# Mixing stage: the scores of a later item between the transposes and the products with the values

## What is computed

```python
s_c = jnp.einsum('bqgrd,bcgd->bqgrc', qg, k_cmp) * scale          # compressed blocks
p_c = masked_softmax(s_c, ...); o_c = einsum(p_c, v_cmp)
_, idx = lax.top_k(score, topk)                                    # 8 blocks of 64 keys per query
p_s = masked_softmax(s_s, (kpos <= qpos)...);  o_s = einsum(p_s, values of those blocks)
p_w = masked_softmax(s_w, wmask);              o_w = einsum(p_w, values of the window of 256)
o = g[..., 0:1] * o_c + g[..., 1:2] * o_s + g[..., 2:3] * o_w
```

## Time and profile before

| | us |
|---|---|
| median of 3 runs | 4092.09 |
| lowest and highest | 4089.07, 4095.11 |
| the profiled execution | 4092.92 |
| its span | 4091.1 |
| TensorE busy in it | 3914.1 (96%) |
| VectorE, GpSimd, ScalarE busy | 2043.8, 1694.0, 1114.4 |

### The profile page before, as it was taken

One profiled execution on the slowest core, in us unless ns is written; L12 is line 12 of the kernel. 1 busy time (PEld: TensorE's weight loads), 2 busy tenths in 40 slices (PEclk: granted clock), 3 DMA queues, 4 the chain that ended last, 5 costly groups with the idle time before them and its releaser, 6 DMA issues. The chain is left out here.

```text
span 4091.1 us, 89056 instructions
## 1 busy us (share of the span) xinstructions
PE 3914.1 (96%) x36904; PEld 3583.7 (88%) x36904; DVE 2043.8 (50%) x4689; ACT 1114.4 (27%) x2470; POOL 1694.0 (41%) x2284
## 2 busy tenths in 40 slices
PE   8998999989999999999999989999899999999997
PEld 8987888876689999999899878888666999999997
DVE  6587544447545424415456864444575454144253
ACT  3153233337731000000212532323477211000001
POOL 5533221126764434434355321221367644344442
PEclk9998999989999999999999999999899999999998
DMA  3254432220032131131323443332200311311312
GB/s 131 87 166 164 115 84 66 84 97 4 16 100 79 46 112 66 42 135 39 111 93 102 149 166 100 82 85 68 95 7 13 123 63 45 135 42 59 118 42 93
DMA packets 201957, 350.13 MB, mean 86 GB/s; under 512 B 72930, under 2 KB 135650, under 8 KB 200674
## 3 DMA queue, kind: packets, MB, share of 16 engines
q1 hardware_dynamic: 201554, 344.44, 26.6%
HBM read 253.18 MB, written 95.90 MB: 85 GB/s over the span
## 5 line engine op out<-in xcount | busy, mean ns | idle before, releaser
L2628 POOL CAST wr_hi<-wr_raw 128x256 fp32r<-128x256 f32 x584 | 263.7, 452 | 906.0 <-PE ps L2663 900.6
L2630 POOL TENSOR_TENSOR wr_lo<-wr_raw,wr_hi 128x256 fp32r<-128x256 f32 x584 | 548.1, 938 | 46.7
L2663 PE MATMUL ps<-xh,wr_hi 128*128 128x384 f32 x2064 | 453.5, 328 | 0.0
L2663 PE MATMUL ps<-xh,wr_lo 128*128 128x384 f32 x2064 | 453.2, 327 | 0.0
L2663 PE MATMUL ps<-xl,wr_hi 128*128 128x384 f32 x2064 | 452.9, 327 | 0.0
L1382 POOL TENSOR_TENSOR rc_CT<-rc_AT,rc_masks 128x256 f32<-128x256 f32 x192 | 138.7, 742 | 602.2 <-DVE rc_AT L1417 451.6
L2663 PEld LDWEIGHTS ps<-xh,wr_hi 128*128 128x128 f32 x2064 | 349.1, 188 | 0.3
L2663 PEld LDWEIGHTS ps<-xl,wr_hi 128*128 128x128 f32 x2064 | 349.0, 188 | 0.0
L2663 PEld LDWEIGHTS ps<-xh,wr_lo 128*128 128x128 f32 x2064 | 348.6, 188 | 0.0
L2716 ACT ACTIVATE de_c<-de_c 128x1088 f32<-128x1088 f32 (+1 forms) x44 | 49.1, 1116 | 1098.2 <-DVE de_c L2812 1098.2
L2663 PE MATMUL ps<-de_mixh,wr_hi 128*128 128x384 f32 (+3 forms) x1440 | 321.6, 331 | 7.9 <-DVE de_mixl L2751 7.9
(11 more groups left out here) (460 smaller groups left out, 8034.3 us busy)
## 6 DMA issues: line engine op xcount, KB each, us to landing
sa_kvp<-in_cache SPq DMA_DIRECT2D x128, 256.0 KB
scr_xres<-de_x SPq DMA_DIRECT2D x56, 544.0 KB, 2.7
de_x<-scr_xres SPq DMA_DIRECT2D x56, 544.0 KB, 3.7
wr_raw<-in_w_gate SPq DMA_DIRECT2D x42, 512.0 KB, 3.5
wr_raw<-in_w_up SPq DMA_DIRECT2D x42, 512.0 KB, 3.5
rc_arbk<-scr_arbk SPq DMA_DIRECT2D x32, 512.0 KB, 4.8
wr_raw<-in_w_down SPq DMA_DIRECT2D x32, 512.0 KB, 3.6
pr_raw<-in_w_rw SPq DMA_DIRECT2D x28, 512.0 KB, 4.2
```

The costliest lines, as they stand in the source:

```text
L2628: pool.tensor_copy(hi[:, k, :], raw[:, k, :]).then_inc(w_hi, 1)
L2630: pool.tensor_tensor(lo[:, k, :], raw[:, k, :], f32(hi[:, k, :]), ALU.subtract).then_inc(w_ready, 1)
L2663: m = pe.matmul(ps[:, (bank + b) * BANK:(bank + b) * BANK + cols], w[rows, k, :], x[rows, k, o:o + cols], start=(k == 0 and i == 0), stop= ...
```

## The change

The one edit is in TensorE's loop. `scores(i + LAG)` stood behind `values(i - 1)` and stands ahead of it:

```diff
@@ -2136,10 +2136,10 @@
             for i in range(-LAG, NI + 2):
                 if 0 <= i < NI:
                     transposes(i)
+                if i + LAG < NI:
+                    scores(i + LAG)
                 if 0 <= i - 1 < NI:
                     values(i - 1)
-                if i + LAG < NI:
-                    scores(i + LAG)
                 yield
```

## The result

| | kernel before | changed kernel |
|---|---|---|
| median of the runs, us | 4093.61 (10 runs, 4086.54 to 4098.73) | 4103.68 (10 runs, 4099.30 to 4106.57) |
| ratio of the times | | 1.0023, 95% interval 1.0013 to 1.0032 |
| profiled execution: span, us | 4091.1 | 4104.8 |

The changed kernel is slower by 0.23%, 10.1 us by the medians and 5.3 to 13.1 by the interval. I measure it from the first score group behind the gap at its start to the end of the last product with the values. Behind that score group every step depends on the one before it, and the moment at which the clock first rose, a little ahead of that score group and not the same in each execution, is left out.

What follows compares the result with a forecast made beforehand. The prediction took the mixing stage to be bound by TensorE's own work. Its terms, 6.5 + 1.9 + 3.4 - 4.0 = +7.8 us on 4092.09, gave 4099.9 us, with a range of 4091 to 4108 for 8 in 10.

Steps and rivals of the forecast that it cites:

- Term A: Diagonal steps: array switches from causal product to values and values to transposes cost 0.13 in 25 steps, +6.5 us both layers.
- The zero price of the new switches: All steps: the new neighbours transposes to scores and scores to values cost nothing in sum over the old ones.
- Rival 4: All steps: the new switches are dear, 0.06 each over 150 steps, 4109 us; plain step above 2.46; chance 0.18.
- the ceiling of 0.17: Stage start: transposes ahead of scores last 0.97, 0.17 over the plain 0.80, an upper bound for that switch.
- Term B: Stage start: first values leave the shadow of a mask wait, next scores are 0.95 late, +1.9 us both layers.
- Term C: Stage start: behind a gap of 3.1 us TensorE's clock falls to half for 3.4 us, +3.4 us both layers.
- Term D: Mixing stage: transposes' waits for GpSimd and L2128's wait for ScalarE shorten, 2.0 per layer, -4.0 us both layers.
- The 7.0 stay: Mixing stage: scores' waits for VectorE's masks, 7.0 us per layer, stay apart from the first of them.
- (1): Stage start: the clock doesn't fall, or falls in one layer only, 4096.5 to 4098 us; chance 0.20.
- (2): Mixing stage: nothing moves, switches are covered by remaining waits and the start is made good, 4092 to 4094 us; chance 0.13.
- (3): Mixing stage: faster, since earlier scores feed VectorE early and mask waits go as well, about 4081 us; chance 0.09.

Runs made afterwards that it cites:

- first step in the old order: Changed kernel, but in the first step that has values they stand ahead of the scores as before: 4095.00 us against 4092.72 of the kernel before, ratio 1.0007.
- two products: Changed kernel with two added products, whose result nobody reads, in the gap ahead of the first moved scores of each layer: 4098.41 us, one execution.
- two kernels without C: Causal product L2107 left out of the changed kernel and of the kernel before: 4079.41 us in the new order, 4081.36 in the old, one execution each.
- kernel with C last: Changed kernel with the causal product L2107 moved behind the values: 4108.11 us, one execution, against 4094.55 of the kernel before.
- run with three products: Changed kernel with three added products, whose result nobody reads, in the gap ahead of the first moved scores of each layer: 4098.56 us, one execution.

## Why the prediction was right, and where its terms were off

Per layer, predicted and measured:

| term | predicted | measured | from |
|---|---|---|---|
| A, switches behind the causal product | +3.25 | +3.0 | busy time, first step in the old order less before |
| B, values out of the wait | +0.95 | +1.9 to +2.05 | two products less first step in the old order |
| C, the clock | +1.7 | +1.6 to +1.7 | changed kernel less two products |
| D, waits that shorten | -2.0 | -2.3 | idle time, first step in the old order less before |
| sum | +3.9 | +4.3 and +4.2 | the stage |

**Term A** held. Behind the gap 31 causal products stand in each layer. In the kernel before 30 of them are followed by a group of 128 by 128, the transposes or one of the two other streams, and the time from start to start is 0.27 or 0.28, but for one of 0.43. In the changed kernel 27 are followed by V and take 0.36 or 0.37, and the four that are followed by L2128, which is 128 by 128 again, take 0.27 or 0.28. So it is the shape of the group behind that counts, and not that the values stand there. C's own groups grew by 2.3 us per layer. The other 0.7 lies in what follows: six transposes behind V take 0.80 and behind C 0.77. I had let the waits for masks cover seven of the 32 steps and priced 25 at 0.13; it is 27 at 0.11. The two kernels without C confirm the size with 3.01.

The Trainium skill's bullet on weight loads ("TensorE: Matmul & The Clock Gate", Part 3, The mechanism: a load overlaps matmuls in flight only where its row group differs) would have had C to T and C to V cost the same. The changed kernel shows 0.37 where V follows and the kernel with C last shows 0.27 where T follows, so the measurement decides against that bullet for this pair. The same section of the Trainium skill also has loads into a background weight buffer pulled ahead, and no row here speaks against that.

**The zero price of the new switches** held to the hundredth: T to T is 2.45 in a plain step against 2.46. Rival 4 fell with it, and the ceiling of 0.17 from the start of the stage was no price, as supposed.

**Term B** is the step that failed, by a factor of two. I counted what the next score group loses, 0.95, and put the last V of the shifted row at nothing, since it falls in the stage's drain and the drain hangs on the last masks. It doesn't: from the start of the last score group to the end of the stage it took 5.41 us before (1147.00 to 1152.41) and takes 5.83 in the changed kernel (1150.34 to 1156.17), so the short V there is paid. The rest comes on the way. A score group is late by L2128 and the first V, 0.95 + 0.81 = 1.76, less the V that now stands behind it instead of ahead. That V is 0.81 at the start and 0.37 at the end, so what is taken off shrinks, and behind the last score group nothing is taken off. TensorE does the same groups in the stage either way: work that leaves a wait is added to its time in full, unless another wait takes it up. Here none did. The remaining 0.1 to 0.3 of the measured 1.9 to 2.05 I can't place.

**Term C** held in place and size. The idle was 3.10 as forecast in layer 1 and 2.75 in layer 2, whose start doesn't repeat that of layer 1 to the tenth, the clock stood at half for 3.4 us in both layers, and without the fall the stage is 1.57 and 1.71 shorter.

The Trainium skill's advice against long idle gaps between bursts, since the clock falls back to half ("TensorE: Matmul & The Clock Gate", Why this matters for your kernels), agrees with this gap. The run with three products shows that the length of one gap isn't the whole rule: there the clock fell behind 1.18 us of idle.

**Term D** had the right mechanism and nearly the right size, out of other parts than I had taken. TensorE is idle for 9.8 us per layer before, behind the first wait, and for 7.6 after. In layer 1 the parts of this moved like this:

- The wait of L2128 for ScalarE fell from 1.5 to 0.5, more than the 0.8 I took.
- The wait for GpSimd fell from 1.9 to 1.1, where I forecast about 1.3. The wait of 1.0 that I had left as it was is gone. Behind it stood a third group of six transposes that lasts 1.19, so there were three per layer and not two:

```profile
1057.16 1.19 PE L2117 MATMUL ps<-cbuf,at_s 128*128 128x128 f32 x6 [1.04 <-POOL at_s L2227]
```

- All three late groups are gone: no group of six transposes in the changed kernel's steady stretch lasts over 1.00. Their idle time lies mostly in pieces too short for the list of waits, and pieces of that kind are what is left for the 0.4 to 0.6 us by which the idle time fell more than the list.
- The masks' waits fell from 5.6 to 5.1, which I had at nothing.
- The wait of the transposes for ScalarE's copies rose from 0.8 to 1.3, which I had at nothing too.

**The masks.** "The 7.0 stay" held roughly: 8.2 with the 3.1 of the start is 5.1 for the others, and 7.0 less 1.44 is 5.6. The kernel with C last shows the mechanism from the other side.

**A sign that came up.** I had written that I would be wrong altogether if VectorE started to wait for the groups of the other two streams. It did, for the compressed branch's scores. VectorE's waits for them, 905 to 1157, before and then in the changed kernel:

```profile
DVE cm_s L2281 <- PE ps L2243: 0.8, 1, 0.8
DVE cm_s L2281 <- PE ps L2243: 5.0, 7, 1.0
```

The sign was chosen too strictly. TensorE's own waits for masks didn't grow with it, and VectorE is busy for 153 of the 241 us, so nothing here shows that these waits cost time. The other sign, a busy time of TensorE that doesn't grow, stayed away.

**The rivals.** The clock fell in both layers (1), the stage didn't stay the same (2), the waits for masks didn't go (3), and the plain step kept its length (4).

**The number.** Per layer term B was about 1.0 too low, and A (0.25 too high) and D (0.3 more saved than forecast) took half of that back. So the sum is nearer than its worst term, and that part is luck: 7.8 forecast for the two layers, 8.5 in the stage, 10.1 by the medians. The changed kernel's 4103.68 lies in the range of 4091 to 4108 but 3.8 above the forecast of 4099.9, outside the 3 us that I gave 0.40. Of the 3.8, 1.5 come from the kernel before, whose median over ten runs is 4093.61 and not 4092.09. The time is beyond the line of 0.2% at 4100.3, which I gave 0.37, less than the 0.55 for no change.

## What to carry to other kernels

In a software pipeline a new order can be free in the steady steps and still lose at the start, where one group stood in the shadow of a long wait: follow what left the shadow, and expect to pay its whole length once per stage, and the clock behind the longer gap besides. Price two neighbours by the pair, not by the group: here only the pair whose tile shape changed cost its 0.1 us. And a new order can be taken for the part of the loop in which its waits win, which gave the shortest stage here, by a gain too small to show in the kernel's time. To read such a change, split the stage into TensorE's busy and idle time between the same two instructions: a switch that costs adds to the first, a wait that shortens takes from the second.

## What the runs showed that I had not expected

The clock fell behind an idle of only 1.18 us in both layers of the run with three products. It stayed full behind 1.17, 1.39 and 1.44 us of idle in others, behind the 1.6 us of the earlier trace rows in the kernel before, and behind the same wait of the same length in the changed kernel, which is this:

```profile
941.44 1.06 PE L2349 MATMUL ps<-ro_rk,ro_rk 128*128 128x8 f32 x8
942.35 1.07 PE L2117 MATMUL ps<-cbuf,at_s 128*128 128x128 f32 x8
944.60 0.92 PE L2099 MATMUL ps<-kwT,qT 64*128 64x384 f32 x4 [1.18 <-DVE at_low L2193]
```

The same groups, one of products with eight columns and one of eight transposes, stand ahead of this wait in the runs with two and with three products, so neither they nor the length of the idle tells when the clock falls. What does isn't settled here.

The clock also fell at places outside the stage that the change doesn't touch. Busy time by stretch of the changed kernel, two stretches at half clock with TensorE busy:

```profile
2577.70:2581.10 3.40, 3.40 (x64) 3.28 (x59) 1.99 (x8) 1.47 (x3) 0.71 (x2) 0.50 0.00 0
2676.70:2680.10 3.40, 3.40 (x52) 3.17 (x54) 2.72 (x11) 1.25 (x2) 0.00 (x0) 0.50 0.03 7
```

Each is worth up to 1.7 us. The profiled execution of the kernel before has no such stretch at these places, and has others elsewhere. Between the two mixing stages (from the end of the last V in layer 1 to the first S behind the gap in layer 2) the changed kernel took 6.1 us longer, which is more than the whole part of the 13.7 that the changed stages leave. How much of the 6.1 the clock makes wasn't worked out. A difference of a few microseconds between single executions has to be placed in the timeline before it is explained.
